# A one-launch transformer kernel: one whole block pair in every feed-forward layer, the last layer's norm by products with ones, two weight sums by accumulating transfers

## The reference, cut to what matters

```python
def rmsnorm(x, g):
    x32 = x.astype(jnp.float32)
    y = x32 * lax.rsqrt(jnp.mean(x32 * x32, axis=-1, keepdims=True) + EPS)
    return (y * g.astype(jnp.float32)).astype(x.dtype)

def conv_ffn(h, w_up, conv_w, conv_b, w_down):          # layers 0 and 1
    u, g = jnp.split(h @ w_up, 2, axis=-1)
    g = causal_dwconv(g, conv_w, conv_b)                # 3 taps and a bias
    return (jax.nn.silu(g) * u) @ w_down
...
        h2 = rmsnorm_2(x, norm2_g[l])                   # layer 2
        g = jnp.einsum('bsd,df->bsf', h2, w_gate[l])
        u = jnp.einsum('bsd,df->bsf', h2, w_up[l])
        x = x + jnp.einsum('bsf,fd->bsd', jax.nn.silu(g) * u, w_down[l])
```

## Time and profile before

| | |
|---|---|
| median of 3 runs (lowest to highest) | 1771.16 us (1771.16 to 1771.86) |
| the profiled execution | 1771.75 us |
| its span in the profile | 1770.0 us |
| mean granted clock of TensorE, share of full | 0.998 |
| busy PE, DVE, ACT, POOL | 99%, 73%, 54%, 12% |
| layer 0, first product, first narrow product of its first step | 260.54 us; two whole pairs later |
| layer 2, first product, first narrow product | 1413.86 us, 1437.47 us |

### The profile page before, as it was taken

The page is one execution under the profiler, slowest core; times in us unless marked ns, Lnnn a source line. Parts: engine busy times, 40 slices in busy tenths (PEclk is TensorE's granted clock), DMA queues, the critical chain, the costliest instruction groups (busy, mean ns, idle before and its releaser), DMA issues.

```text
span 1770.0 us, 26240 instructions
## 1 busy us (share of the span) xinstructions
PE 1759.2 (99%) x10680; PEld 1527.0 (86%) x10680; DVE 1295.2 (73%) x1794; ACT 950.3 (54%) x1442; POOL 203.7 (12%) x223
## 2 busy tenths in 40 slices
PE   9999999999999999999999999999999999999998
PEld 7877788999999887787899999977777899999997
DVE  6878568888786765646888787689767487776765
ACT  6645444655555544755465555552567455454454
POOL 0001220110111200002011110103001101111110
PEclk9999999999999999999999999999999999999999
DMA  6221223654545342212364554443221236555442
GB/s 250 72 90 66 71 95 108 155 138 137 143 127 136 89 158 99 96 49 93 98 178 113 154 127 140 111 119 107 73 96 50 103 99 151 135 143 143 109 141 73
DMA packets 61623, 205.19 MB, mean 116 GB/s; under 512 B 7344, under 2 KB 9520, under 8 KB 53184
## 3 DMA queue, kind: packets, MB, share of 16 engines
q1 hardware_dynamic: 38832, 162.55, 27.6%
q0 software_dynamic: 17280, 31.46, 10.0%
q10 hardware_dynamic: 5392, 9.51, 1.7%
HBM read 169.38 MB, written 2.13 MB: 97 GB/s over the span
## 4 chain that ended last, share of the span: by engine, by line
PE 89%; DVE 6%; ACT 3%; issue 1%; DMA 1%; ACTq 0%; DVEq 0%; POOL 0%; SPq 0%
PE ps L1846 31%; PE ps L1497 17%; PE ps L1872 16%; PE ps L1411 6%; PE ps L1536 4%; PE ps L1659 2%; PE ps L1704 2%; PE ps L1556 2%; PE ps L1684 2%; PE ps L1895 2%; DVE WL L2531 1%; PE ps L1743 1%; PE ps L1724 1%; PE ps L1913 1%; ACT WH L1986 1%
## 5 line engine op out<-in xcount | busy, mean ns | idle before, releaser
L1846 PE MATMUL ps<-hH,WH 128*128 128x256 f32 x896 | 253.9, 283 | 0.8 <-ACT held L2063 0.8
L1846 PE MATMUL ps<-hH,WL 128*128 128x256 f32 x896 | 254.0, 283 | 0.0
L1846 PE MATMUL ps<-hL,WH 128*128 128x256 f32 x896 | 253.9, 283 | 0.0
L2553 DVE TENSOR_TENSOR WL<-raw,WH 128x1024 fp32r<-128x1024 f32 x138 | 168.2, 1220 | 113.1 <-ACT WH L1997 113.1
L2531 DVE TENSOR_TENSOR WL<-raw,WH 128x1024 fp32r<-128x1024 f32 (+1 forms) x137 | 167.5, 1260 | 89.3 <-ACT WH L1986 88.9
L1497 PE MATMUL ps<-hH,WH 128*128 128x512 f32 x528 | 208.7, 395 | 0.3 <-DVE WL L2531 0.3
L1497 PE MATMUL ps<-hH,WL 128*128 128x512 f32 x528 | 205.9, 390 | 0.0
L1497 PE MATMUL ps<-hL,WH 128*128 128x512 f32 x528 | 205.9, 390 | 0.0
L3288 POOL DMA_DIRECT2D X<-sq x120 | 104.8, 959 | 866.3 <-ACT sq L2052 864.4
L1846 PE MATMUL ps<-TH,WL 128*128 128x256 f32 x672 | 190.5, 283 | 0.0
L1846 PE MATMUL ps<-TL,WH 128*128 128x256 f32 x672 | 190.4, 283 | 0.0
(11 more groups left out here) (442 smaller groups left out, 3897.7 us busy)
## 6 DMA issues: line engine op xcount, KB each, us to landing
raw<-in_wall SPq DMA_DIRECT2D x166, 512.0 KB, 4.3
raw<-in_wall SPq DMA_DIRECT2D x65, 1024.0 KB, 4.8
X<-sq POOLq DMA_DIRECT2D x120, 256.0 KB, 4.0
bias<-in_bias ACTq DMA_DIRECT2D x12, 256.0 KB, 3.0
raw<-in_wall SPq DMA_DIRECT2D x8, 256.0 KB, 7.0
X<-in_xt SPq DMA_DIRECT2D x8, 256.0 KB, 7.8
CB<-rows ACTq DMA_DIRECT2D x8, 256.0 KB, 3.4
out_y<-X SPq DMA_DIRECT2D x8, 256.0 KB, 2.2
```

Source lines behind the costliest of these rows:

```text
L1846: mm = e.matmul(ps[b][:, 256 * u:256 * u + 256], ww[:, p, 128 * u:128 * u + 128], x, start=(opens and p == 0 and u == 0 and n == 0), stop= ...
L2553: e.tensor_tensor(L, chunk_src(c), H.bitcast(F32), ALU.subtract).then_inc(*mark("wl", "c", c))
```

## The change

Layers 0 and 1 begin with one whole pair, as layer 2 did, and their second pair becomes a step. All three layers have the norm by products with ones. The four parts of TH/TL are made ahead of the first weight conversion of the first step, without sums between them. In layers 0 and 1 the taps and silus of the whole pair (`wt0`) stand behind q5, `wy0` and the first `wu0` behind q6, the second `wu0` behind q3, `wlast` behind q7; in layer 2 they stay where they were. The sums for q5 and q6 of the first step of each layer are formed by five transfers from HBM on POOL's queue, a plain one into each of the two buffers and then adding ones, in three rounds put behind the output tiles 1, 3 and 5; a round's adding transfers wait for the one before into the same buffer to land. The blocks themselves are still loaded, since q1, q7 and q4 need them. Besides, the marks of POOL's first memsets share one semaphore.

```diff
-WHOLE = (2, 2, 1)
+WHOLE = (1, 1, 1)
...
+DMA_SUMS = {5: ("A21", "A22"), 6: ("A11", "A21", "A22")}
+DMA_ROUNDS = (((0, 5, 0), (1, 6, 0)), ((0, 5, 1), (1, 6, 1)), ((1, 6, 2),))
+DMA_AT = {1: 0, 3: 1, 5: 2}
...
         for key in dict.fromkeys(SEQUENCE[i]):
-            c = {"key": (i,) + key, "i": i, "sum": None, "unit": None}
+            c = {"key": (i,) + key, "i": i, "sum": None, "unit": None, "dma": False}
             if key[0] == "q":
                 _, s, q = key
                 parts = [ROLE[i, b, s] for b in BLOCKS[q]]
+                c["dma"] = s == WHOLE[i] and q in DMA_SUMS
                 if q in SUMS:
                     c["sum"] = {6: [(i, "q", s, 5)], 3: [(i, "q", s, 6)]}.get(q, []) + parts
                     c["place"] = {5: 0, 6: 1, 3: 0, 7: 1}[q]
...
         for n, when, key in ([(c["unit"], at, ("wl", "c", x))] if c["unit"] is not None else
-                             [(y, at - 1.5, ("wg", "sum", x)) for y in c["sum"] if not isinstance(y, tuple)]):
+                             [(y, at - 1.5, ("wg", "sum", x)) for y in c["sum"]
+                              if not c["dma"] and not isinstance(y, tuple)]):
...
-ROW_NORMS = ("ffn0", "kv", "ffn1")
+ROW_NORMS = ("ffn0", "kv", "ffn1", "n2")
...
-                        if CHUNKS[c]["sum"]:
+                        if CHUNKS[c]["sum"] and not CHUNKS[c]["dma"]:
                             put("wsum", c)
                         now["summed"] = c + 1
...
             if m:
                 for x in (0, 1) if m == 1 else (m,):
                     tile_done("res_norm", stage, x, nrm)
+            if m in DMA_AT:
+                put("wdma", WINO_OF[nrm], DMA_AT[m])
...
                 tile_done("res_norm", stage, m, nrm)
                 for x in T_SUMS.get(m, ()):
                     put(x[0], WINO_OF[nrm], x[1])
+                if m in DMA_AT:
+                    put("wdma", WINO_OF[nrm], DMA_AT[m])
...
-        def sum_ahead(i):
-            c = now["summed"]
-            while CHUNKS[c]["i"] < i or not CHUNKS[c]["sum"]:
-                c += 1
-            put("wsum", c)
-            now["summed"] = c + 1
-
...
-        if st in ROW_NORMS:
-            put("row_split", st)
+        put("row_split", st)
         n = take()
-        if st in ROW_NORMS:
-            put("sqrt_table", st)
+        put("sqrt_table", st)
         whole("g", 0, n)
-        if st in ROW_NORMS:
-            put("wtS", i, 1)
-            half(1, n, 0)
-            put("row_sums", st, 60)
-            put("wtL", i, 1)
-            half(1, n, 1)
-            put("row_inverse", st)
-            put("wtB", i, 2)
-            put("wtS", i, 2)
-        else:
-            put("rstd_first", st, 61)
-            put("wtS", i, 1)
-            put("wtL", i, 1)
-            put("wtB", i, 2)
-            put("wtS", i, 2)
-            whole("g", 1, n)
-            put("rstd_second", st)
+        put("wtS", i, 1)
+        half(1, n, 0)
+        put("row_sums", st, 61 if i == 2 else 60)
+        put("wtL", i, 1)
+        half(1, n, 1)
+        put("row_inverse", st)
+        put("wtB", i, 2)
+        put("wtS", i, 2)
         done.add(n)
-        if WHOLE[i] == 1:
-            sum_ahead(i)
         put("wtL", i, 2)
         put("wtB", i, 3)
         if WHOLE[i] == 1:
             put("wtS", i, 3)
-            sum_ahead(i)
             put("wtL", i, 3)
...
         done.add(n)
         if WHOLE[i] == 1:
             conv_ahead(len(UNITS))
-            for m in (0, 1):
-                put("wt0", f"g{i}", m)
-            put("wy0", i, 0)
+            if i == 2:
+                for m in (0, 1):
+                    put("wt0", f"g{i}", m)
+                put("wy0", i, 0)
         conv_ahead(len(UNITS))
...
         if WHOLE[i] == 2:
             later([], [("wu0", f"u{i}", 3)], [("wt7", i)], [("wlast", i, 1)])
+        elif i == 2:
+            later([("wt7", i)], [("wu0", f"u{i}", 0)], [("wu0", f"u{i}", 1)], [("wlast", i, 0)])
         else:
-            later([("wt7", i)], [("wu0", f"u{i}", 0)], [("wu0", f"u{i}", 1)], [("wlast", i, 0)])
+            later([("wt7", i)], [("wt0", f"g{i}", 0), ("wt0", f"g{i}", 1)], [("wy0", i, 0), ("wu0", f"u{i}", 0)],
+                  [("wu0", f"u{i}", 1)], [("wlast", i, 0)])
...
+        def summed(c):
+
+            c = CHUNKS[c]
+            if c["dma"]:
+                x = c["place"]
+                return (s_wsum[x] if ev.sems else None), 16 * len(DMA_SUMS[c["key"][3]]) * (c["i"] + 1)
+            return at("wg", "sum", CHUNK_AT[c["key"]])
...
                 elif what == "cconv":
                     c = a[0]
                     if CHUNKS[c]["sum"]:
-                        w.wait_ge(*at("wg", "sum", c))
+                        w.wait_ge(*summed(c))
...
+                elif what == "wdma":
+                    i, r = a
+                    w.wait_ge(*at("out", OUT_OF[i], 0))
+                    for x, pn, n in DMA_ROUNDS[r]:
+                        if n:
+                            w.wait_ge(s_wsum[x] if ev.sems else None, 16 * (len(DMA_SUMS[pn]) * i + n))
+                        y = ROLE[i, DMA_SUMS[pn][n], WHOLE[i]]
+                        src = wall[:, WOFF[y]:WOFF[y + 1]]
+                        if n:
+                            e.dma_start(Wsum[x][:, :], src, accum_op=ALU.add).then_inc(s_wsum[x], 16)
+                        else:
+                            e.dma_start(Wsum[x][:, :], src).then_inc(s_wsum[x], 16)
 
...
-                     "n2": [("vev", "fv", 2, 1)], "last": [("spread", "n2")]}
+                     "last": [("vev", "fv", 2, 1)]}
```

More of the change, by code:

```diff
@@ L1189, in program @@
         s_part = [sem(f"part{i}") for i in range(2)]
+        s_wsum = [sem(f"wsum{i}") for i in range(2)]
         s_mem = [sem(f"mem{i}") for i in range(4)]
@@ L1966, in scalar @@
                         e.dma_start(mrA[:, 2 * i:2 * i + 2, :], src[:, 2 * i:2 * i + 2, :]).then_inc(s_mem[i], 16)
-                    w.wait_ge(*at("eps", 1))
+                    w.wait_ge(*at("set", "eps1"))
                     e.activation(small[:, 62:63], small[:, 60:61], ACT.Copy).then_inc(*mark("wh", "warm"))
@@ L2538, in vector @@
                         if isinstance(y, tuple):
-                            w.wait_ge(*at("wg", "sum", CHUNK_AT[y]))
+                            w.wait_ge(*summed(CHUNK_AT[y]))
                             src.append(Wsum[CHUNKS[CHUNK_AT[y]]["place"]][:, :])
@@ L3195, in gpsimd @@
                     e.memset(gw[:, :, :], 0.0).then_inc(*mark("set", "gw0"))
-                    e.memset(small[:, 60:61], 1e-6).then_inc(*mark("eps", 0))
-                    e.memset(small[:, 63:64], 1e-11).then_inc(*mark("eps", 2))
-                    e.memset(small[:, 61:62], 1e-5).then_inc(*mark("eps", 1))
+                    e.memset(small[:, 60:61], 1e-6).then_inc(*mark("set", "eps0"))
+                    e.memset(small[:, 63:64], 1e-11).then_inc(*mark("set", "eps2"))
+                    e.memset(small[:, 61:62], 1e-5).then_inc(*mark("set", "eps1"))
                     for n, (c, size) in enumerate(V_ONES):
@@ L3202, in gpsimd @@
                     for i, j in ((0, 0), (1, 2), (2, 3)):
-                        e.tensor_copy(KB[:, i, :], K[:, j, :]).then_inc(*mark("KB", i))
+                        e.tensor_copy(KB[:, i, :], K[:, j, :]).then_inc(*mark("set", "KB", i))
                 elif what == "fence":
```

## The result

The changed kernel takes **1795.49 us** (median of 4 runs, 1794.65 to 1796.79), beside 1771.18 for the kernel before on the same chip: ratio 1.0136, interval 1.0121 to 1.0151, so 24.3 us slower. The forecast was 1786, +14.8, with a range to 1794. The direction held, the size did not. The profiled execution took 1796.79 (span 1794.8).

The account below looks back on a forecast made before the run. The kernel was taken to be bound by TensorE's instruction stream, without slack behind any wait. Terms -4.6 + 4.0 + 13.8 + 1.6 = +14.8 us gave 1786 us by the median, the forecast's own range 1781 to 1790, overall 1775 to 1794.

Parts of the forecast that it names:

- the one on the transfers: Five more 512 KB transfers per layer on POOL's queue: cost TensorE from 0 to rival B's price, taken as 0.
- rival B: POOL is held waiting for transfers to land, each chain to q1 1.5 us later: +4.5, 1790.5 us; chance 0.07.
- Rival A: Clock falls to its lower level behind q7's wait: +2.8 us in each of two layers, 1791.5 us; chance 0.13.
- TensorE's saving: Fewer or narrower products: -3.2 us from pairs in layers 0 and 1, -1.35 from the last layer's norm, together -4.6.
- The waits at q1: TensorE waits for q1's low weights at each layer's start: 0.45, 2.2 and 1.35 us, together 4.0.
- Layers 0 and 1 behind q1: Per layer, q7 waits 3.9 us for q6's copy, the first down piece 3.0 more for FL; 13.8 in all.
- The last layer: q6 waits 1.6 us for the copy of q1's result, late behind q3's high half and the silu table load.
- C: Rival: all the lateness is hidden and only the -4.6 us saving stays: 1766.6 us, faster; chance 0.12.
- D: Rival: only the waits at q1 and in the last layer are real: +1.0, 1772 us, no change; chance 0.08.
- the prediction's estimate: A plain 512 KB transfer from POOL's queue would take an estimated 3.2 us; not used in the sum.

Follow-up runs that it names:

- e6: Changed kernel with its five transfers per layer issued by SyncE's queue as plain copies, the two weight sums left out: 1785.09 us.
- e1: Changed kernel without the new transfers, the two weight sums made by VectorE again: 1786.55 us.
- e4: Changed kernel with idle products, their results overwritten, put ahead of the late products where TensorE waits: 1793.24 us.
- e7: Changed kernel with the row norm's reciprocal moved behind the conversions of q1 and q5: 1798.24 us.
- e10: Changed kernel with q4 of the first step ahead of the first down piece in all layers: 1794.61 us.
- e12: Kernel before with the last layer's new norm alone, that layer's reciprocal behind q1's and q5's conversions and its silus behind the copy of q1's result: 1773.49 us.
- e2: Kernel before with one part of the change alone, the last layer's norm by products with ones: 1773.43 us.
- e9: Changed kernel with taps, silus and what hangs on them behind ScalarE's copy of q6's result in layers 0 and 1: 1798.83 us.
- e13: Changed kernel without the four VectorE tap operations in the first step of layers 0 and 1: 1792.15 us.
- e8: Changed kernel with each layer's first down piece moved behind q1 and q5 of the second step: 1799.72 us.

## Why the prediction was wrong in size and right in kind

**The step that failed** is the one on the transfers: "So the sums cost TensorE nothing, from 0 up to the price in rival B, and I take 0: POOL's additions to the row sum have gaps". I asked whether POOL had time for them. It had; VectorE had not. With the issue between two additions VectorE's two-input operations stand 2.6 us longer in a layer (the changed kernel's rows against e6's). This term of the sum, taken as 0, measured 8.9 us by e1, more than rival B's price of 4.5, and that rival's mechanism, POOL waiting for a landing, cost nothing that the traces show. The Trainium skill (SBUF — State Buffer, 🔬 SBUF: two separate sides) says of the pair of ports that VectorE and GpSimd share, for a VectorE operation with two SBUF inputs and a GpSimd operation that reads SBUF, that "whichever ... starts first gets the pair for the whole instruction; the other fully blocks", and that transfers and compute ports are disjoint. The second agrees: T7f takes 1.52 us with as many bytes from SyncE's queue. The first agrees as far as POOL's additions go, behind which T7f ends in both kernels; that POOL's issue of a transfer holds VectorE as well is what the 2.99 us show here. The trace of before already had the sign: beside the two additions from 248.71 its T7f takes 1.5 us and not 0.48. I didn't look.

**The second miss** is the clock. Rival A had its kind but, for the changed kernel, not its place: it was laid behind q7, at 2.8 us in each of two layers. There it fell in q1 and in the down piece, and e4 prices it at 2.3 us in all. Behind q7 it fell in e1, e6, e7 and e10. e1 has three falls and the changed kernel five, so the transfers may have a part in it; since the place of a fall changes between runs with the same gap, that is not shown.

**TensorE's saving** (-4.6) stands uncontradicted: the page has 10810 - 10680 = 130 more products, which are +336 narrow, -192 wide, and -14 by the norm (16 narrow products with K gone, two with ones added: eight go in each of the two groups, not four as the prediction says). The norm's part shows in e12, where q1 stands 22.21 us behind t0 and not 23.61 as before. The pairs' part never shows, since the first step of layers 0 and 1 goes by VectorE and ScalarE.

**The waits at q1** were forecast as 0.45, 2.2 and 1.35: measured 2.15, 3.20, 2.16 with the transfers. In e6, with neither POOL nor VectorE making the sums, they are 0.57, 2.33 and 1.44, each within 0.15 us of the forecast. In e1 they are 0.70, 3.36 and 1.59. The one that is off there, in layer 1, stands behind a longer wait of VectorE for the small transfer of the earlier trace rows: 2.73 us in e1 and 3.31 in the changed kernel, for 1.64 before and 1.65 in e6. Why it lands later in some kernels is open.

**Layers 0 and 1 behind q1** (6.9 each): 24.18 - 17.28 = 6.9 twice. The split was 3.9 and 3.0; it came as 1.92 of wait for the held copy, some 1.7 of slow products ahead of it, which hid in the same wait (in e10, where the clock stays up until q7, that wait is 3.41), and a gap of 3.29 before the piece, 3.0 of it idle. The piece's own 1.7 us came on top.

**The last layer** (1.6): the excess between q1 and the piece is 19.04 - 17.28 = 1.76. In the changed kernel no wait at q6 can be seen, but only because slow products behind q1's gap fill the same time: with the clock up TensorE waits 1.49 us there in e4, and 1.43 in e1 and e2, and the piece starts 19.0 us behind q1 in all of them. The number and the cause were both right.

**What the waits mean.** C and D asked whether they are real. They are, and they are not independent: the first down piece of layer 0 starts 49.4 us behind t0 in the changed kernel, 50.1 in e7, 49.5 in e9, 47.2 in e1, 47.1 in e6 and 46.5 in e13; TensorE wants it at 22.21 + 17.28 = 39.5. Reordering moved a wait from one product to the next; only work or hold-ups taken from VectorE (e1, e6, e13) brought the piece forward. Whether a different split between VectorE and ScalarE could make the whole pair pay was not tried.

## What to carry to other kernels

When work leaves a bound engine, follow the queue that feeds it from start to end and sum it: a product that starts earlier gains nothing if the last of its chain stays. A transfer issued by POOL is priced on VectorE as well: look at what VectorE has open while POOL issues. And read waits in a row as one: remove the first and see by how much the last one moves.

## What the runs showed that I had not expected

The issue of two 512 KB transfers between two additions of POOL makes VectorE's operations there longer: 1.1 us where they are plain, 1.5 where they accumulate. The accumulating ones land 6.9 to 9.8 us after their issue (median 7.8, where the prediction took its chances from 4.0 for 256 KB), the plain ones of the same queue in 3.8 to 5.8 (4.3, where the prediction's estimate was 3.2):

```profile
DMA to landing us min/median/max: 6.9/7.8/9.8
...
DMA to landing us min/median/max: 3.8/4.3/5.8
```

At the starts of the feed-forward layers in these runs the granted clock fell behind every gap of 2.76 us or more, to 0.50 at the lowest. Behind shorter ones it went both ways. In q1 of layer 0 it fell at 2.54 us (changed kernel) and 2.56 (e8), and stayed up at 2.52 (e9), 2.53 (e13) and 2.55 (e10); in layer 1 it fell at 2.19 (q6 in e7) and 2.02 (e10, third step) and stayed up at 2.71 (q1 in e6). So no length read from one run can be taken as the limit. The Trainium skill (TensorE: Matmul & The Clock Gate, HAM oscillation — how this bites in real kernels) counts on longer idle gaps than 2.54 us before the clock falls; here the measurement decides. The same piece of 24 wide products took 5.46 us at the full clock, 7.14 in the changed kernel behind a gap of 3.29 us, and 8.23 in e13 behind the same gap.
